# Turning the attention probabilities: TensorE transposes replaced by 32x32 block transposes on VectorE and a trip through DRAM

## What is computed

```
SEQ, DIFF_HEADS, DIFF_DH, DIFF_VD, Q_BLOCK, CHUNK = 512, 4, 64, 128, 128, 64
...
        visible = (k_pos[None, :] // CHUNK) <= (q_pos[:, None] // CHUNK)
        logits = jnp.einsum('bqhmd,bkhmd->bhmqk', q_blk, k).astype(f32) * scale + bias[None, :, None]
        logits = jnp.where(visible, logits, NEG_INF)
        p = jax.nn.softmax(logits, axis=-1)
        attn = p[:, :, 0] - lam * p[:, :, 1]
        return jnp.einsum('bhqk,bkhe->bqhe', attn.astype(v.dtype), v)
```

## Time and profile before

| | us |
|---|---|
| median of 3 runs | 1756.7 (1756.33 to 1756.97) |
| span of the profiled execution | 1754.5 |
| PE busy | 1746.8 |
| DVE busy | 1269.8 |
| ACT busy | 744.8 |
| POOL busy | 487.5 |

### The profile page before, as it was taken

The page is one execution under the profiler, slowest core; times in us unless marked ns, Lnnn a source line. Parts: engine busy times, 40 slices in busy tenths (PEclk is TensorE's granted clock), DMA queues, the critical chain, the costliest instruction groups (busy, mean ns, idle before and its releaser), DMA issues.

```text
span 1754.5 us, 21902 instructions
## 1 busy us (share of the span) xinstructions
PE 1746.8 (100%) x8231; PEld 1454.1 (83%) x8231; DVE 1269.8 (72%) x1688; ACT 744.8 (42%) x967; POOL 487.5 (28%) x204
## 2 busy tenths in 40 slices
PE   9999999999999999999999999999999999999998
PEld 7888888888888888888888888888888888888888
DVE  7998767573678777577779787665746797585585
ACT  4234654343564443343432345543445544343343
POOL 4453000103034244444133620010030333444440
PEclk9999999999999999999999999999999999999999
DMA  6532222322322332232231312223222223322321
GB/s 216 192 120 73 103 103 96 127 90 97 119 82 87 122 116 79 98 115 85 107 144 72 145 69 106 103 97 120 97 97 96 97 99 118 121 72 97 120 75 70
DMA packets 30698, 185.97 MB, mean 106 GB/s; under 512 B 3709, under 2 KB 6013, under 8 KB 10241
## 3 DMA queue, kind: packets, MB, share of 16 engines
q1 hardware_dynamic: 28380, 172.71, 27.4%
q0 software_dynamic: 1648, 11.54, 1.7%
q10 hardware_dynamic: 564, 0.33, 0.1%
HBM read 179.25 MB, written 7.68 MB: 107 GB/s over the span
## 4 chain that ended last, share of the span: by engine, by line
PE 96%; DVE 2%; issue 1%; ACT 1%; POOL 0%; DVEq 0%; POOLq 0%; ACTq 0%
PE ps L1640 28%; PE ps L1656 28%; PE ps L1641 28%; PE ps L1582 2%; PE ps L1576 2%; PE ps L1575 2%; PE ps L1739 1%; PE ps L1759 1%; DVE merged L1202 1%; DVE x_tl L985 1%; PE ps L1751 0%; PE ps L1670 0%; PE ps L1891 0%; PE ps L1884 0%; PE ps L1885 0%
## 5 line engine op out<-in xcount | busy, mean ns | idle before, releaser
L1640 PE MATMUL ps<-x_hd,w_hd 128*128 128x512 f32 x1568 | 612.8, 391 | 0.2
L1641 PE MATMUL ps<-x_tl,w_hd 128*128 128x512 f32 x1568 | 610.4, 389 | 0.0
L566 POOL TENSOR_TENSOR w_tl<-raw,w_hd 128x2048 fp32r<-128x2048 f32 x79 | 366.1, 4634 | 534.4 <-ACT w_hd L684 400.7
L684 ACT ACTIVATE w_hd<-raw 128x2048 fp32r<-128x2048 f32 (+2 forms) x159 | 298.2, 1876 | 324.8 <-PE ps L1641 240.3
L1656 PE MATMUL ps<-x_hd,w_tl 128*128 128x512 f32 x1568 | 373.4, 389 | 0.0
L1640 PEld LDWEIGHTS ps<-x_hd,w_hd 128*128 128x128 f32 x1568 | 294.4, 188 | 62.5 <-issue 0.8
L1656 PEld LDWEIGHTS ps<-x_hd,w_tl 128*128 128x128 f32 x1568 | 294.1, 188 | 61.0
L1641 PEld LDWEIGHTS ps<-x_tl,w_hd 128*128 128x128 f32 x1568 | 294.4, 188 | 60.3
L1640 PE MATMUL ps<-ring_hd,w_hd 128*128 128x512 f32 (+1 forms) x640 | 241.1, 381 | 0.0
L1641 PE MATMUL ps<-ring_tl,w_hd 128*128 128x512 f32 (+1 forms) x640 | 239.8, 379 | 0.0
L1347 DVE SCALAR_TENSOR_TENSOR merged<-merged 128x512 f32<-128x512 f32 x44 | 183.3, 4166 | 20.7 <-ACT merged L684 20.3
(11 more groups left out here) (227 smaller groups left out, 1646.1 us busy)
## 6 DMA issues: line engine op xcount, KB each, us to landing
raw<-units SPq DMA_DIRECT2D x154, 1024.0 KB, 4.8
bias_t<-bias_tiles POOLq DMA_DIRECT2D x8, 256.0 KB, 5.5
cg<-mem_t POOLq DMA_DIRECT2D x2, 1024.0 KB, 6.8
resid<-x_t POOLq DMA_DIRECT2D x1, 2048.0 KB, 8.2
resid_dram<-resid POOLq DMA_DIRECT2D x1, 2048.0 KB, 9.1
resid<-resid_dram POOLq DMA_DIRECT2D x1, 2048.0 KB, 8.8
out<-resid SPq DMA_DIRECT2D x7, 256.0 KB, 2.7
resid<-x_t SPq DMA_DIRECT2D x3, 512.0 KB, 9.0
```

Of the source, the lines that this page charges most:

```text
L566: line.done(pool.tensor_tensor(w_tl[:, k % 2, :], raw[:, k % 2, :], w_hd[:, k % 2, :].bitcast(F32), ALU.subtract), of_unit("tail", g))
L684: line.done(act.activation(out, in_, func, **kw), *labels)
L1640: pe.matmul(dst, w_hd[:, slot, w], hd[:, src, :], start=kc == 0, stop=False)
L1641: i = pe.matmul(dst, w_hd[:, slot, w], tl[:, src, :], start=False, stop=False)
```

## The change

Job C is gone. Behind `combine`, VectorE issues one instruction on the head's 128 x 1280 probabilities, which turns each 32x32 block where it stands and writes it to `s_sb[:, 1]` with key blocks innermost, so that neighbours of a row of a turned block lie 10 elements apart. SyncE sends that to DRAM in one transfer (640 KB, two buffers in turn), waits for its landing and reads it back in four transfers of 160 KB, one for each band of 32 partitions: runs of 320 elements (1280 bytes) from four bands of DRAM rows, by which the 32x32 blocks change places. `att_t` is now `s_sb[:, 0]`, seen as [partition, tile, query] with a step of 10 elements between queries. Job D waits for the four landings instead of ScalarE's copies, and TensorE's later waits on those copies become waits on VectorE's score instructions. SyncE does this ahead of the load of unit 19 + 3h (`TURN_AT`).

```diff
--- before.py
+++ after.py
@@ -233,7 +233,6 @@
 for _h in range(HEADS):
     ATT.setdefault(ATT0 + 3 * _h, []).append(("A", _h))
     ATT.setdefault(ATT0 + 3 * _h + 1, []).append(("B", _h))
-    ATT.setdefault(ATT0 + 3 * _h + 2, []).append(("C", _h))
 for _h in range(HEADS):
     ATT.setdefault(ATT0 + 3 * _h + 3, []).insert(0, ("D", _h))
     ATT.setdefault(ATT0 + 3 * _h + 4, []).insert(0, ("E", _h))
@@ -252,8 +251,7 @@
 QK_TAILS = {21: 3}
 QK_AT = {0: (4, 6), 1: (5, 7), 3: (2, 3)}
 YA_ROUNDED = CLN + 5
-AO = [0, 512, 896, 1152]
-AT_AT = [(4, 0), (5, 0), (6, 0), (6, 256)]
+TURN_AT = {ATT0 + 3 * _h + 6: _h for _h in range(HEADS)}
 
 
 C_IN, C_OUT = (0, 1, 4, 5), (2, 3, 0, 6)
@@ -385,7 +383,7 @@
         u_sb, vn = merged[:, 0:4, :], merged[:, 4:8, :]
         v_sb = sb("v_sb", [P, TB, BR])
         s_sb = sb("s_sb", [P, 2, 1280])
-        att_t = s_sb[:, 1, :]
+        att_t = s_sb[:, 0, :].rearrange("p (q t) -> p t q", q=P)
         strip = s_sb[0:HEADS, 0, 0:NREL + 1]
         tmp = sb("tmp", [P, 4, S])
         sq = sb("sq", [P, 2, S])
@@ -431,6 +429,7 @@
         bias_rows = nc.dram_tensor("bias_rows", (HEADS, P * (NREL + 1)), F32).ap()
         bias_tiles = nc.dram_tensor("bias_tiles", (HEADS, P, S), F32).ap()
         wsbs_dram = nc.dram_tensor("wsbs_dram", (DEPTH, 2, P, S), F32).ap()
+        att_dram = nc.dram_tensor("att_dram", (2, P, 1280), F32).ap()
         resid_dram = nc.dram_tensor("resid_dram", (P, KD, S), F32).ap()
 
 
@@ -447,6 +446,7 @@
             sem("strip_out"), sem("rows_out"), sem("tiles_out"), sem("masked_out"), sem("wsbs_out"))
         wsbs_in, resid_out, resid_in, mem_in = (
             sem("wsbs_in"), sem("resid_out"), sem("resid_in"), sem("mem_in"))
+        att_in, att_out = sem("att_in"), sem("att_out")
         bias_in = [sem("bias_in0"), sem("bias_in1")]
         out_sent = sem("out_sent")
         vector_waited, gpsimd_waited = sem("vector_waited"), sem("gpsimd_waited")
@@ -525,7 +525,20 @@
                     for h in range(HEADS):
                         sp.dma_start(bias_tiles[h, 0:CHUNK, S - CHUNK:S], neg_tile[:]).then_inc(masked_out, 16)
 
+            def turn(h):
+                n = line.part * HEADS + h
+                sp.wait_ge(vector_done, line.at(f"turned{h}"))
+                sp.dma_start(att_dram[n % 2], s_sb[:, 1, :]).then_inc(att_out, 16)
+                sp.wait_ge(att_out, 16 * (n + 1))
+                for b in range(4):
+                    sp.dma_start(s_sb[32 * b:32 * b + 32, 0, :].rearrange("i (a f) -> i a f", a=4),
+                                 att_dram[n % 2].rearrange("(a i) f -> i a f", a=4)[:, :, 320 * b:320 * b + 320]
+                                 ).then_inc(att_in, 16)
+
             for g in range(2, TOTAL):
+                line.begin(g // NU)
+                if g % NU in TURN_AT:
+                    turn(TURN_AT[g % NU])
 
                 sp.wait_ge(gpsimd_done if tail_by_pool(g - 2) else vector_done, line.at(of_unit("tail", g - 2)))
                 sp.dma_start(raw[:, g % 2, :], units[g]).then_inc(weights_in[g % 2], 16)
@@ -850,9 +863,6 @@
                                 view = s_sb[:, m, SO[qb]:SO[qb] + P * (qb + 1)]
                                 op(view, view, ACT.Exp, (f"exp{job}_{h}",), (f"neg{job}_{h}",),
                                    bias=mneg[:, 4 * m + qb:4 * m + qb + 1], accum_out=sm[:, 4 * m + qb:4 * m + qb + 1])
-                        elif job == "C":
-                            for (bank, c0), o, w in (((4, 0), 0, 512), ((5, 0), 512, 384), ((6, 0), 896, 384)):
-                                op(att_t[:, o:o + w], ps[:, bank, c0:c0 + w], labels=(f"att{h}",), needs=(f"C{h}",))
                         elif job == "D":
                             for qb in range(TB):
                                 op(junk[:], tmp[:, 2, P * qb:P * qb + P], ACT.Square, (f"oss{h}",), (f"o_raw{h}",),
@@ -1097,7 +1107,7 @@
                     bank, c0 = SC_AT[m, qb]
                     w = P * (qb + 1)
 
-                    free = (f"C{h - 1}", f"D{h - 1}") if h else ()
+                    free = (f"D{h - 1}",) if h else ()
                     op(lambda: dve.tensor_tensor_reduce(
                         out=s_sb[:, m, SO[qb]:SO[qb] + w], in0=ps[:, bank, c0:c0 + w],
                         in1=bias_t[:, h % 2, S - w:S], scale=1.0, scalar=-3.0e38, op0=ALU.add, op1=ALU.max,
@@ -1117,7 +1127,10 @@
                     w = P * (qb + 1)
                     s0, s1 = s_sb[:, 0, SO[qb]:SO[qb] + w], s_sb[:, 1, SO[qb]:SO[qb] + w]
                     op(lambda: dve.scalar_tensor_tensor(s0, s1, rc[:, 4 + qb:5 + qb], s0, ALU.mult, ALU.add),
-                       f"probs{h}", independent=min(qb, 1))
+                       independent=min(qb, 1))
+
+                op(lambda: dve.transpose(s_sb[:, 1, :].rearrange("p (b i t) -> p t b i", b=4, i=32),
+                                         s_sb[:, 0, :].rearrange("p (t b i) -> p t b i", b=4, i=32)), f"turned{h}")
 
             def conv_taps(taps):
                 for i, t in taps:
@@ -1720,7 +1733,7 @@
                     if job == "B":
                         pe.wait_ge(vector_done, line.at(f"sc_freeA_{h}"))
                     elif h:
-                        pe.wait_ge(scalar_done, line.at(f"att{h - 1}"))
+                        pe.wait_ge(vector_done, line.at(f"sc_freeB_{h - 1}"))
                     if h in QK_AT:
                         pe.wait_ge(vector_done, line.at(f"k_tail{h}"))
                         q, key = (QK_AT[h][n] for n in range(2))
@@ -1741,22 +1754,12 @@
                                 if (m, qb) == (0, 1) and p == len(parts) - 1:
                                     line.done(i, f"A_first{h}")
                     line.done(i, f"{job}{h}")
-                elif job == "C":
-                    pe.wait_ge(vector_done, line.at(f"probs{h}"))
-                    for kb in range(TB):
-                        bank, c0 = AT_AT[kb]
-                        for qb in range(kb, TB):
-                            c = c0 + P * (qb - kb)
-                            s0 = SO[qb] + P * kb
-                            i = pe.transpose(ps[:, bank, c:c + P], s_sb[:, 0, s0:s0 + P], ident[:])
-                    line.done(i, f"C{h}")
                 elif job == "D":
-                    pe.wait_ge(scalar_done, line.at(f"att{h}"))
+                    pe.wait_ge(att_in, 64 * (l * HEADS + h + 1))
                     pe.wait_ge(vector_done, line.at(f"ot{h - 1}" if h else "c_norm3"))
                     for qb in range(TB):
                         for kb in range(qb + 1):
-                            c = AO[kb] + P * (qb - kb)
-                            i = pe.matmul(misc[:, P * qb:P * qb + P], att_t[:, c:c + P], v_sb[:, kb, P * h:P * h + P],
+                            i = pe.matmul(misc[:, P * qb:P * qb + P], att_t[:, SO[qb] // P + kb], v_sb[:, kb, P * h:P * h + P],
                                           start=kb == 0, stop=kb == qb)
                     line.done(i, f"D{h}")
                 else:
@@ -1856,7 +1859,7 @@
                         attention(job, h)
                     if k == 26:
 
-                        pe.wait_ge(scalar_done, line.at("att3"))
+                        pe.wait_ge(vector_done, line.at("sc_freeB_3"))
                         column_sums("mem", (), mem_sums, MB)
                     if k == 27:
                         pe.wait_ge(vector_done, line.at("ot3"))
```

## The result

The changed kernel takes 1765.7 us (median of 5, 1764.88 to 1766.05) against 1756.7 us before: ratio 1.0052, interval 1.004 to 1.0064. It is 9.0 us slower, where 8.7 us faster was forecast. The profiled executions differ by 9.3 us of span.

A forecast was written before the change was run, and what follows sets the result against it. The prediction took TensorE, busy 1746.8 of 1754.5 us, as the bound. Its terms were -8.7 us for the removed transposes and 0 for all others, giving 1748.0 from 1756.7; likeliest case 1747 to 1751, 8-in-10 range up to 1765.

The forecast's parts named there:

- Changed in TensorE's value products: Term for reading the stationary tile at a 40-byte step: taken as 0, with bounds up to +17.8 us.
- rival A: In each head's value products the stationary tile loads too slowly: 1760.9 at 192 ns, 1765.8 at 223 ns; chance 0.42.
- Removed from TensorE: Term for the ten probability transposes a head, eight heads, taken off TensorE's chain: -8.7 us, all gain.
- Added to VectorE: Term for one 128x1280 block transpose a head: 1.4 us, covered by 1.8 us of slack, so 0.
- the output turn: TensorE's turn of head 0's normalised output from VectorE, taken as the tightest work behind the block transpose: 2.9 us slack.
- Rival C: VectorE's strided write in the block transpose is slow, 3.0 us, the rest as forecast: 1750.4 us; chance 0.06.
- Added between probabilities and value product: Term for the path through DRAM: 10.2 us with the block transpose, under 11.1 allowed at head 0, so 0.
- Removed from ScalarE: Term for 24 copies out of PSUM, 12.7 us, no longer made: counted as 0 because ScalarE is no bound.
- moved past SyncE's queue: Term for the later weight load, issued at about 197.4 instead of 194.75: 8 us of slack, so 0.

The follow-up runs named there:

- e3: The kernel before, with only the value products' stationary tiles read at a step of 4 elements (16 bytes): 1774.84 us.
- e4: The kernel before, with only the value products' stationary tiles read at a step of 2 elements (8 bytes): 1757.3 us.
- e10: The kernel before, with only the value products' stationary tiles read at a step of 3 elements (12 bytes): 1766.15 us.
- e9: The changed kernel with the value products' stationary tiles read densely and VectorE's block transpose also writing densely: 1747.88 us.
- e2: The changed kernel with only the value products' stationary tiles read densely, the block transpose still writing with its step: 1749.45 us.
- e5: The changed kernel with tiles stored in pairs (8-byte step), two block transposes, four transfers out in 256-byte runs; attention still computed correctly: 1751.2 us.
- e6: The changed kernel plus one ScalarE copy of 128x1280 a head, from stepped to dense order, ahead of the value products: 1762.55 us.
- e8: The kernel before, with one of the three 512-column products of every weight unit reading its stationary tile at a 40-byte step: 1822.31 us.

## Why the prediction was wrong

- *Changed in TensorE's value products: "I take 0".* This step failed. The term is +17.6 us. Its upper bound, "twice today's step, +111.5 x 160 = +17.8", was the measured case, and rival A at 223 ns gave 1765.8 against 1765.7 measured. The reasoning that led to 0 was that records with one column repeated run at 110 ns, like dense ones, so "addressing is not what limits a load". A step of zero reads one place again and again; it says nothing of a step that reaches a new 16 bytes with each element (e3, e4, e10). The nearest row in kind was on the wrong side of what decides. The weight load's 192 ns, hidden in 111.5, was no sign of room either: at 322 ns shown the pace was 222.
- *The Trainium skill against the trace.* By the Trainium skill, "Advanced Engine Details and Errata", section SBUF Cachelines, a step that leaves 16 bytes with each access is penalised, and the trace agrees: 221.5 ns a record for 111.5. The prediction's estimate for it, 214 ns, gave 8 us on the slow side; measured +9.0. No row of before spoke against it, since none had such a step; rival A was given 0.42 and the forecast, which rests on the dense rows and those with a column repeated, 0.43. The prediction had the mechanism and the price, and chose the other.
- *Removed from TensorE: -8.7.* Right. Dense throughout (e9) the kernel gains 8.6.
- *Added to VectorE: 1.4 us, covered.* The row taken (1.12 ns an element) fits a dense write (1.18), not this one: 2.58 us. Of the 1.8 us of slack that were counted, 2.58 leaves 0.8 us uncovered, twice, 1.6 us in all. That is what e2 pays over e9 (1.57), though the wait falls on the gates' copy out of PSUM (line 1277; 1264 before), not on the output turn (line 1765 of before) to which the prediction put it. That the amount fits is chance: before, that copy ends at 202.65 + 1.29 = 203.94 and TensorE comes to its next unit at 206.89, a slack of 2.95 us beside the 2.9 of the output turn, which the prediction took for the tightest. In the changed kernel itself it costs nothing, since TensorE is late by more; it was hidden behind the larger mistake. Rival C had its size nearly right. The two rows, from the timeline and from the chain of the kernel before:

```profile
202.65 1.29 DVE L1264 TENSOR_TENSOR tmp<-ps,r 128x512 f32<-128x512 f32 x2
```
```profile
206.89 0.43 PE ps L1640
```

- *Added between probabilities and value product: covered.* Right: no wait on DRAM. The legs were 8.8 us by estimate; out took 2.9 us and not 3.75, the last landing about 3.2 + 1.3 for the issues ahead of it and not 4.75, so some 7.7. The block transpose took back what the legs gave. Head 0 keeps about 1 us, as said, and e5 shows what lies beyond: 2.8 us more for the transfer out, 1.0 less for the block transpose, and TensorE waits at head 0.
- *Removed from ScalarE: 0, moved past SyncE's queue: 0.* Right: TensorE's wait for ScalarE's rounding is 0.9 us in three pieces, as before. The unit's load is issued at 198.78, not at 197.4.
- *The range* reached up to 1765 and missed by 0.7: it was cut within rival A, though the price of twice the dense pace, 1765.8, was known and the rival had 0.42.

## What to carry to other kernels

A layout is paid for by whoever reads it: for each operand whose step changes, look at how many elements it takes out of 16 bytes, whether TensorE loads it or streams it or VectorE writes it, and don't let rows of dense or zero-step instructions stand in for it. If a transfer can leave elements in pairs (f32), the step is nearly free, and what that costs is more and shorter runs in DRAM. A repair that adds a wait at a place where TensorE has none pays the wait, and may pay a lower clock behind it: in e6, behind waits of 4.9 and 4.5 us, the granted clock was 0.50; in e5, behind waits of 1.0 and 1.6 us, it was 1.00.

## What the runs showed that was not expected

- A 12-byte step costs 172 ns a record, between 118 at 8 bytes and 227 at 16: the price follows the share of reads that are alone on their 16 bytes.
- The moving operand at a 16-byte step costs the same 226 ns a record while its loads stay at 208.
- Beside 512-column matmuls a stationary step of 40 bytes still costs 30 ns a record (e8), 65.9 us in this kernel.
- ScalarE copies from a 40-byte step at 2574 ns for 1280 elements (e6's group of eight copies), 2.01 ns an element, the rate of VectorE's write at that step:

```profile
L698 ACT ACTIVATE s_sb<-s_sb 128x1280 f32<-128x1280 f32 x8 | 20.6, 2574 | 30.0 <-DMA s_sb<-att_dram 29.9
```

- The same 640 KB in 256-byte runs land in 12.8 us as one transfer whose outermost dimension is 4, and within 5.8 us as four transfers. The DMA share is 0.25 in the first, and 0.26 in the other transfer here whose outermost dimension is 4.
